# Forget attention on one core: a turn's dense filling in two parts instead of three

## The chip, the cores and the metric

One core of a Trainium2 chip runs the whole program in one launch. The metric is the time of that launch on the device in microseconds (us), as a median over runs. TensorE is called PE in the profile (PEld are its weight loads), VectorE DVE, ScalarE ACT, GpSimd POOL and SyncE SP.

## What is computed

Two blocks in a row on x of 1024 tokens by 1024 channels, in fp32: the first is a pooling mixer beside sliding-window attention, the second has eight heads of forgetting attention (causal, with a decay from cumulated log gates), eight heads of chunk-band attention, gates, and a feed-forward part. The change touches the two attentions of the second block and the projections that run between them:

```python
def forgetting_attention(q, k, v, log_f):
    c = jnp.cumsum(log_f, axis=-1)
    def block(args):
        qi, ci, i = args
        sc = jnp.einsum('bhqd,bhkd->bhqk', qi, k, preferred_element_type=jnp.float32)
        sc = sc * scale + ci[..., None] - c[:, :, None, :]
        sc = jnp.where(mask, sc, NEG)
        p = jax.nn.softmax(sc, axis=-1).astype(v.dtype)
        return jnp.einsum('bhqk,bhkd->bhqd', p, v)
...
def second_block(x, ...):
        h = rms_norm(x, norm1[l])
        proj = h @ w_in[l]
        qa, ka, va, fa, qc, kc, vc, gates = jnp.split(proj, SPLITS, axis=-1)
        o_a = from_heads(forgetting_attention(...))
        o_b = from_heads(chunk_band_attention(...))
        g_a, g_b = jnp.split(jax.nn.sigmoid(gates), N_BRANCH, axis=-1)
        merged = g_a * (o_a @ w_branch_a[l]) + g_b * (o_b @ w_branch_b[l])
        x = x + merged @ w_out[l]
        h2 = rms_norm(x, norm2[l])
        x = x + jnp.square(jax.nn.relu(h2 @ w_up[l])) @ w_down[l]
    return rms_norm(x, final_norm)
```

## The kernel before

**Precision.** A dense product is made of matmuls on halves: an operand is split into a high part (rounded to fp32r, by ScalarE) and a low part (the rest, by VectorE), and high x high, high x low and low x high are added in one PSUM bank. One *dense step* is such a group of three matmuls, 128x128 by 128x512, for one of eight slices of the inner dimension (`dense` is a generator that yields after each).

**The work of the attention.** The 16 heads are taken as eight pairs, 0 to 3 with the chunk band ("band pairs"), 4 to 7 with the causal mask and the forget gates ("causal pairs"). A *slot* is one head and one block of 128 queries, 128 in all; two slots make a `Step`, whose key blocks lie in groups of up to four blocks. A pair has 16 slots and 8 steps. `STEP_ORDER` is (3, 0, 2, 1): a step with many keys is followed by one with few.

**What sets TensorE's order.** The loop over *turns* in `tensor_program` writes it by hand. A turn holds

1. the scores of its slot (two fp32r matmuls for each part of up to four key blocks; in the causal pairs a small bf16 matmul adds the mask), into the banks 2 and 3 by turns;
2. filling, the first part (place 0);
3. the transposes (*turning*) of one visit's groups: `turn_weights` transposes up to four 128x128 blocks of the normed rows into the bank 5 or 6. It waits for `normed` (ScalarE scaled the rows) and for the low half (`plow`) of the group that had the bank before. A step's groups are turned in two visits, in two turns (`spread` is 2);
4. filling, the second part (place 1);
5. `products`: the groups turned in the turn before, times V, into the bank 4 or 7. They wait for those groups' `plow`;
6. filling, the third part (place 2).

The filling is the dense work of the next pairs' k, q and v and of three gates, from the generator `att_fill`. `take` adds a part of the turn's quota to a running credit and issues one dense step for each whole one. `att_quota` shares out 48 steps for a pair (37 for the last) over its slots by their number of keys. The transposes of v (`turn_v`) are issued inside a dense product.

**The other engines** follow the same turns, each in its own fixed order. ScalarE (`scalar_program`): the exponential of the turn's slot, the high half of the groups turned in this turn (`p_high`), the scaling (`normed`), half of a finished output, the evacuation of what dense work ended in this turn's three places, the high half of newly loaded weights. VectorE (`vector_program`): the low half of the groups turned in the turn before (`p_low`), add and maximum of the scores, an output, the low halves of k and q that ended in the turn before, the reciprocal (`one over`), the low half of weights. Both handle all that ended in a turn together, whatever its place.

**Names in the profile.** In this stretch dense matmuls read `b<-Yr,ringr`, scores `b<-Xr`, the mask `b<-maskb,identb`, products `b<-Wr,Xr`, transposes `b<-identf,Wf` (L93). `Wr<-b` on L97 is the high half of a turned group, `Wr<-b,Wr` on L101 its low half; `ringr<-stage` are the weights' halves; `Wf<-Wf,st` is the exponential on L98 and the scaling on L97; `Wf<-b,Wf` on L112 is the add with maximum; `st` are the small statistics.

Of the kernel before, what the change touches and what calls it, by code (L numbers as in the profile page):

```python
# [21 lines left out]
POOL_SLOT = (0, 1, 3, 2)  # L22
STEP_ORDER = (3, 0, 2, 1)
SLAB_OF_MERGED = (3, 1, 2, 4, 5, 6, 7, 0)
FILL = (0.3, 0.3, 0.4)
HALVES = ((0, 0), (1, 0), (0, 1))


# [510 lines left out]
def block(t):  # L539
    return slice(t * P, t * P + P)  # L540
# [11 lines left out]
def att_quota(slot):  # L552
    keys_of = band if slot.step.pair < 4 else causal
    total = 2 * sum(len(keys_of(i)) for i in range(NT))
    quanta = ATT_QUOTA if slot.step.pair < 7 else LAST_QUOTA
    return quanta * (len(slot.keys) + FIXED_KEYS) / (total + 16 * FIXED_KEYS)


def tensor_program(pe, m, at, note, units, swa, att):
# [125 lines left out]
    def take(steps, credit, quota):  # L685
        credit[0] += quota
        while credit[0] >= 1:
            credit[0] -= 1
            next(steps, None)

    def swa_fill():
        yield from dense("k", m.X, x_ready[1], 1, (0, 1))
        yield from dense("q0", m.X, x_ready[1], 1, (0, 1))
        yield from dense("ag0", m.X, x_ready[0], 0, (0, 1))
        yield from dense("v", m.X, x_ready[1], 1, (0, 1))
        for n in dense("ag0", m.X, x_ready[1], 1, (0, 1)):
            if n == 2:
                turn_v("s", m.vT1, 1)
            yield n
        for name in ("q1", "ag1", "q2", "ag2", "q3", "ag3", "u3", "pg3"):  # L700
            for h in range(2):
                yield from dense(name, m.X, x_ready[h], h, (0, 1))

    def turn_weights(stage, step, g, e_block, rooms, banks):
        b = banks[turn_count[0] % len(banks)]
        turn_count[0] += 1
        r = room_count[0] % len(rooms)
        room_count[0] += 1
        pe.wait_ge(*at["normed", stage, step.n])
        pe.wait_ge(*at[freed[b]])  # L710
        blocks = step.groups[g][0]
        for i, which in enumerate(blocks):
            sent = pe.transpose(m.banks[b][:, block(i)], e_block(step, which), m.identf[:])
        sent.then_inc(m.p_t, ("pturned", stage, step.n, g))
        note.bank["pturned", stage, step.n, g] = b
        note.room["pt", stage, step.n, g] = r
        note.room_free["pt", stage, step.n, g] = note.room.get(("pt", stage, r))
        note.room["pt", stage, r] = ("prod", stage, step.n, g)
        freed[b] = ("plow", stage, step.n, g)

    def products(stage, step, g, v_of, v_keys, rooms, base, b, room_free):
        pe.wait_ge(*at["plow", stage, step.n, g])
        if g == 0:
            for key in v_keys:
                pe.wait_ge(*at[key])
            pe.wait_ge(*at[room_free])
        r = rooms[note.room["pt", stage, step.n, g]]
        every = step.groups[g][1]
        for i, (key, c0, width, oc) in enumerate(every):
            for l in range(2):  # L730
                sent = pe.matmul(m.banks[b][:, base + oc:base + oc + width], v_of(key), r[:, l, c0:c0 + width],
                                 g == 0 and i == 0 and l == 0, g == len(step.groups) - 1 and i == len(every) - 1 and l == 1)
        sent.then_inc(m.p_v, ("prod", stage, step.n, g))
        note.bank["o", stage, step.n] = b

    place[0] = ("swa", -1, 0)
    credit = [0.0]
    steps = swa_fill()
    take(steps, credit, FIRST_STEPS)
    out_at = [0]  # L740
    for t, turn in enumerate(swa):
        quota = SWA_TAIL if turn.slot is None else FIRST_QUOTA if t < 4 else SWA_QUOTA
# [16 lines left out]
        place[0] = ("swa", t, 0)  # L759
        take(steps, credit, FILL[0] * quota)  # L760
        for step, g in turn.turned:
            def e_block(step, which):
                key, j = which
                i = step.n % 8
                at_ = j * 256 + (key - max(0, i - 1)) * P
                return m.e1[step.n % 3][:, at_:at_ + P]
            turn_weights("swa", step, g, e_block, m.pt1, TURN_BANKS)
        place[0] = ("swa", t, 1)
        take(steps, credit, FILL[1] * quota)
        for step, g in turn.applied:  # L770
# [8 lines left out]
        place[0] = ("swa", t, 2)  # L779
        take(steps, credit, FILL[2] * quota)  # L780
    place[0] = ("swa", len(swa), 0)
# [140 lines left out]
    def att_fill():  # L922
        names = [f"{x}2{n}" for n in range(1, 8) for x in "kqv"] + ["gb0", "ga0", "gb1"]
        valued = None
        for name in names:
            for h in range(2):
                for step in dense(name, m.Y, h2_ready[h], h, (0, 1)):
                    if valued is not None and step == 3:
                        turn_v(valued[0], m.vT2, valued[1])
                        valued = None  # L930
                    yield step
                if name[0] == "v":
                    valued = int(name[2]), h

    place[0] = ("att", -1, 0)
    steps = att_fill()
    credit = [0.0]
    take(steps, credit, LEAD)
    for t, turn in enumerate(att):
        quota = ATT_TAIL  # L940
        if turn.slot is not None:
            s = turn.slot
            n, j = s.step.pair, s.step.head
            quota = att_quota(s)
            q, k, _ = m.pair_rooms(n)
            for h in range(2):
                pe.wait_ge(*at["free", f"q2{n}", h])
                pe.wait_ge(*at["kdup", f"k2{n}", h])
            for x, ks in enumerate(s.parts):
                b = SCORE_BANKS[score_count[0] % 2]  # L950
                score_count[0] += 1
                pe.wait_ge(*at[freed[b]])
                kc = slice(ks[0] * P, ks[-1] * P + P)
                o = m.banks[b][:, 0:len(ks) * P]
                diag = n >= 4 and ks[-1] == s.i
                pe.matmul(o, q[:, j, block(s.i)], k[:, j, 0, kc], True, False)
                sent = pe.matmul(o, q[:, j, block(s.i)], k[:, j, 1, kc], False, not diag)
                if diag:
                    sent = pe.matmul(m.banks[b][:, block(len(ks) - 1)], m.identb[:], m.maskb[:], False, True)
                sent.then_inc(m.p_s, ("score", "att", s.n, x))  # L960
                note.bank["score", s.n, x] = b
                freed[b] = ("top", "att", s.n, x)
            if s.n == 111:
                ring.reached["att6_done"] = [("score", "att", s.n, len(s.parts) - 1)]
        place[0] = ("att", t, 0)
        take(steps, credit, FILL[0] * quota)
        for step, g in turn.turned:
            def e_block(step, which):
                key, jj = which
                keys_of = band if step.pair < 4 else causal  # L970
                first = keys_of(2 * step.a)
                c = first.index(key) if jj == 0 else len(first) + keys_of(2 * step.a + 1).index(key)
                return m.E2[0 if step.a >= 2 else 1][:, block(c)]
            turn_weights("att", step, g, e_block, m.pt2, ATT_TURN_BANKS)
        place[0] = ("att", t, 1)
        take(steps, credit, FILL[1] * quota)
        for step, g in turn.applied:
            v, j = m.pair_rooms(step.pair)[2], step.head
            products("att", step, g, lambda key: v[:, key, j, :, :].rearrange("p l c -> p (l c)"),
                     [("v", step.pair, h) for h in range(2)], m.pt2, 0, ATT_OUT_BANKS[step.n % 2],  # L980
                     ("oadd", "att", step.n - 2) if step.n > 1 else freed[ATT_OUT_BANKS[step.n % 2]])
            if g == len(step.groups) - 1:
                if step.n == 55:
                    ring.reached["v6_done"] = [("prod", "att", 55, g)]
        place[0] = ("att", t, 2)
        take(steps, credit, FILL[2] * quota)
        if turn.slot is None or turn.slot.step.pair == 7:
            ring.prepare(place[0], 1)
    for x in range(2):
# [1993 lines left out]
def build(nc, x, w_in, pool_w, pool_scale, attn_sinks, w_out, norm_pre, norm_post, norm1_2, w_in_2,  # L2983
# [11 lines left out]
    for program in (tensor_program, scalar_program, vector_program, gpsimd_program, sync_program):  # L2995
        program(Lane(None, at), m, at, note, units, swa, att)
# [50 lines left out]
```

## Time and profile before

| what | value |
|---|---|
| median of 3 runs | 1842.23 us (1841.41 to 1843.25) |
| the profiled execution, own time | 1841.51 us |
| its span, first to last instruction | 1839.4 us |
| PE busy | 1814.0 us, 99% of the span, 8937 matmuls |
| PEld busy | 1507.7 us, 82% |
| DVE busy | 1158.0 us, 63% |
| ACT busy | 922.2 us, 50% |
| chain that ended last, share on PE | 87% |
| mean granted clock of TensorE | 0.998 |

The chain is followed back from the last instruction, at each step to what released it. "Busy" adds up the intervals in which an engine works; of a matmul the start is measured and the end is modelled, and neighbours overlap, so TensorE's pace is read from start to start. In the timeline, equal instructions in a row are merged to one line with their count, and a bracket at the end is the idle time ahead of it with what released it. The attention of the second block runs from about 413 to 900 us.

### The profile page before, as it was taken

Reading aid. Unit: us, or ns where it says so; the run is one execution under the profiler, and the core shown is the slowest. Engines: PE = TensorE matmul, PEld = TensorE weight load, DVE = VectorE, ACT = ScalarE, POOL = GpSimd, SP = SyncE. Lnnn points to the kernel's source line nnn. Section 1 sums busy time; section 2 is a strip of 40 time slices with the busy share of each in tenths; the row PEclk is TensorE's granted clock in tenths of the full one; section 3 lists DMA queues with packets and bytes.
Section 4 is the critical chain, followed back from the end, with each engine's and each line's share of the span. In section 5 each row is a group of like instructions: output and inputs, shape, how many; then the busy total and the mean of one; then the engine's idle time right before and its main releaser. Section 6 shows DMA issues by size and latency. Waiting matters only on the chain.

```text
span 1839.4 us, 23494 instructions
## 1 busy us (share of the span) xinstructions
PE 1814.0 (99%) x8937; PEld 1507.7 (82%) x8937; DVE 1158.0 (63%) x2220; ACT 922.2 (50%) x1629; POOL 90.8 (5%) x165
## 2 busy tenths in 40 slices
PE   8999999999999999999999999999999999999998
PEld 6888888878888888887888888888888888888887
DVE  5788854546666666666532224488665567687877
ACT  5556433347777777777511114245555555433343
POOL 4111100000000000000000000000000000000000
PEclk9999999999999999999999999999999999999999
DMA  5411115333222223122321114324445367554422
GB/s 173 127 35 30 47 46 161 110 88 84 69 72 54 64 76 78 54 66 78 92 55 46 51 53 137 115 75 144 148 145 168 129 216 259 183 186 170 177 96 115
DMA packets 160034, 196.41 MB, mean 107 GB/s; under 512 B 9441, under 2 KB 114473, under 8 KB 156466
## 3 DMA queue, kind: packets, MB, share of 16 engines
q1 hardware_dynamic: 154034, 182.30, 30.8%
q0 software_dynamic: 5888, 12.62, 3.0%
q8 instruction: 70, 1.15, 0.3%
q14 instruction: 42, 0.34, 0.1%
HBM read 139.25 MB, written 49.34 MB: 103 GB/s over the span
## 4 chain that ended last, share of the span: by engine, by line
PE 87%; DVE 6%; ACT 3%; issue 2%; DMA 0%; POOL 0%; SPq 0%; DVEq 0%; POOLq 0%; ACTq 0%
PE b L86 64%; PE b L90 19%; PE b L93 4%; DVE Wf L112 1%; DVE Wr L101 1%; ACT Wf L98 1%; DVE ringr L101 1%; ACT Wf L97 1%; DVE Xr L101 1%; ACT Xr L97 1%; ACT Wr L97 1%; ACT ringr L97 0%; DMA stage<-in_w_in_dram 0%; DVE Wf L101 0%; DVE st L119 0%
## 5 line engine op out<-in xcount | busy, mean ns | idle before, releaser
L86 PE MATMUL b<-Yr,ringr 128*128 128x512 f32 x1920 | 507.7, 400 | 0.0
L86 PE MATMUL b<-Xr,ringr 128*128 128x512 f32 (+1 forms) x1608 | 390.5, 390 | 0.9 <-DVE Wr L101 0.6
L86 PEld LDWEIGHTS b<-Yr,ringr 128*128 128x128 f32 x1920 | 340.3, 189 | 54.4
L86 PEld LDWEIGHTS b<-Xr,ringr 128*128 128x128 f32 x1608 | 292.4, 189 | 56.0 <-issue 1.2
L98 ACT ACTIVATE Wf<-Wf,st 128x640 f32<-128x640 f32 (+3 forms) x192 | 125.2, 652 | 162.6 <-DVE st L116 66.0
L101 DVE TENSOR_TENSOR Wf<-Wf,b 128x512 f32<-128x512 f32 x160 | 108.6, 684 | 117.1 <-PE b L86 70.2
L101 DVE TENSOR_TENSOR ringr<-stage,ringr 128x1024 fp32r<-128x1024 f32 x79 | 97.2, 1234 | 134.3 <-ACT ringr L97 133.9
L112 DVE CUSTOM_DVE_ANT_0 Wf<-b,Wf 128x256 f32<-128x256 f32 (+3 forms) x256 | 118.3, 490 | 70.2 <-PE b L86 69.8
L97 ACT ACTIVATE Wf<-b 128x512 f32<-128x512 f32 (+3 forms) x231 | 114.9, 498 | 86.0 <-PE b L86 60.5
L86 PE MATMUL b<-Xr 128*128 128x512 f32 (+3 forms) x672 | 150.3, 354 | 0.0
L86 PEld LDWEIGHTS b<-Xr 128*128 128x128 f32 x672 | 123.0, 188 | 21.3
L93 PE MATMUL b<-identf,Wf 128*128 128x128 f32 (+1 forms) x809 | 119.2, 275 | 10.8 <-DVE Wr L101 5.1
L101 DVE TENSOR_TENSOR Wr<-b,Wr 128x512 fp32r<-128x512 f32 (+2 forms) x186 | 112.8, 624 | 25.1 <-ACT Wr L97 22.4
L93 PEld LDWEIGHTS b<-identf,Wf 128*128 128x128 f32 (+1 forms) x809 | 94.5, 140 | 41.3 <-ACT Wf L97 12.2
L97 ACT ACTIVATE Wf<-Wf 128x512 f32<-128x512 f32 (+1 forms) x114 | 71.2, 625 | 107.7 <-DVE Wf L101 104.8
L86 PE MATMUL b<-Yr,Xr 128*128 128x512 f32 x528 | 123.3, 391 | 0.0
L97 ACT ACTIVATE ringr<-stage 128x1024 fp32r<-128x1024 f32 x80 | 84.1, 1055 | 66.6 <-PE b L86 62.8
L86 PEld LDWEIGHTS b<-Yr,Xr 128*128 128x128 f32 x528 | 98.7, 188 | 20.3
L97 ACT ACTIVATE Wf<-Wf,st 128x640 f32<-128x640 f32 (+7 forms) x128 | 93.9, 733 | 9.2 <-DVE st L119 9.0
L97 ACT ACTIVATE Wr<-b 128x512 fp32r<-128x512 f32 (+2 forms) x186 | 95.4, 535 | 5.5 <-PE b L93 4.3
L86 PEld LDWEIGHTS b<-Wr,Xr 128*128 128x128 f32 x608 | 86.0, 189 | 8.1
L97 ACT ACTIVATE Xr<-b 64x512 fp32r<-64x512 f32 (+1 forms) x108 | 62.9, 592 | 52.4 <-PE b L93 39.9
(174 smaller groups left out, 2453.8 us busy)
## 6 DMA issues: line engine op xcount, KB each, us to landing
stage<-in_w_in_dram SPq DMA_DIRECT2D x58, 512.0 KB, 4.0
scratch_u<-Wf SPq DMA_DIRECT2D x80, 256.0 KB, 4.1
Wf<-scratch_u SPq DMA_DIRECT2D x14, 1024.0 KB, 4.7
stage<-scratch_u SPq DMA_DIRECT2D x13, 1024.0 KB, 4.8
stage<-in_w_up_dram SPq DMA_DIRECT2D x24, 512.0 KB, 4.3
stage<-in_w_out_dram SPq DMA_DIRECT2D x16, 512.0 KB, 3.5
scratch_x<-Wf SPq DMA_DIRECT2D x16, 512.0 KB, 2.7
Xr<-Xr POOLq DMA_DIRECT2D x32, 256.0 KB, 3.4
```

What stands on the lines that cost most here:

```text
L86: return self.send(lambda e: e.matmul(o, w, a, start=start, stop=stop))
L90: return self.send(lambda e: e.matmul(o, w, a, start=False, stop=stop, skip_group_check=True))
L93: return self.send(lambda e: e.transpose(o, a, ident))
L97: return self.send(lambda e: e.activation(o, a, fn, bias=bias, scale=scale))
L98: return self.send(lambda e: e.activation(o, a, fn, bias=bias, scale=scale, accum_out=acc))
L101: return self.send(lambda e: e.tensor_tensor(out=o, in0=a, in1=b, op=op))
L112: return self.send(lambda e: e.tensor_tensor_reduce(out=o, in0=a, in1=b, scale=1.0, scalar=LOWEST, op0=ALU.add, op1=ALU.max, accum_out=top))
```

## The change

In the attention of the second block (`att`) the filling of a turn has two parts: 0.6 of the quota ahead of the transposes, none between transposes and products, 0.4 behind the products. The first block's attention (`swa`) keeps `FILL`. The middle place still exists, but nothing is issued in it.

```diff
--- before.py
+++ after.py
@@ -22,7 +22,7 @@
 POOL_SLOT = (0, 1, 3, 2)
 STEP_ORDER = (3, 0, 2, 1)
 SLAB_OF_MERGED = (3, 1, 2, 4, 5, 6, 7, 0)
-FILL = (0.3, 0.3, 0.4)
+FILL, ATT_FILL = (0.3, 0.3, 0.4), (0.6, 0.4)
 HALVES = ((0, 0), (1, 0), (0, 1))
 
 
@@ -963,7 +963,7 @@
             if s.n == 111:
                 ring.reached["att6_done"] = [("score", "att", s.n, len(s.parts) - 1)]
         place[0] = ("att", t, 0)
-        take(steps, credit, FILL[0] * quota)
+        take(steps, credit, ATT_FILL[0] * quota)
         for step, g in turn.turned:
             def e_block(step, which):
                 key, jj = which
@@ -973,7 +973,6 @@
                 return m.E2[0 if step.a >= 2 else 1][:, block(c)]
             turn_weights("att", step, g, e_block, m.pt2, ATT_TURN_BANKS)
         place[0] = ("att", t, 1)
-        take(steps, credit, FILL[1] * quota)
         for step, g in turn.applied:
             v, j = m.pair_rooms(step.pair)[2], step.head
             products("att", step, g, lambda key: v[:, key, j, :, :].rearrange("p l c -> p (l c)"),
@@ -983,7 +982,7 @@
                 if step.n == 55:
                     ring.reached["v6_done"] = [("prod", "att", 55, g)]
         place[0] = ("att", t, 2)
-        take(steps, credit, FILL[2] * quota)
+        take(steps, credit, ATT_FILL[1] * quota)
         if turn.slot is None or turn.slot.step.pair == 7:
             ring.prepare(place[0], 1)
     for x in range(2):
```

On TensorE this moves instructions. In the band pair 1, around two turns (a dense step is `b<-Yr,ringr` x3), the order was:

```order
L86 MATMUL b<-Xr 128x128 x2
L93 MATMUL b<-identf,Wf 128x128 x8
L86 MATMUL b<-Yr,ringr 128x512 x3
L86 MATMUL b<-Wr,Xr 128x256 x2
L86 MATMUL b<-Wr,Xr 128x128 x2
L86 MATMUL b<-Xr 128x256 x2
L86 MATMUL b<-Yr,ringr 128x512 x3
L93 MATMUL b<-identf,Wf 128x128 x2
L86 MATMUL b<-Yr,ringr 128x512 x3
L86 MATMUL b<-Wr,Xr 128x256 x8
```

and at the same place it is now:

```order
L86 MATMUL b<-Xr 128x128 x2
L86 MATMUL b<-Yr,ringr 128x512 x3
L93 MATMUL b<-identf,Wf 128x128 x8
L86 MATMUL b<-Wr,Xr 128x256 x2
L86 MATMUL b<-Wr,Xr 128x128 x2
L86 MATMUL b<-Xr 128x256 x2
L86 MATMUL b<-Yr,ringr 128x512 x6
L93 MATMUL b<-identf,Wf 128x128 x2
L86 MATMUL b<-Wr,Xr 128x256 x8
```

In both turns one dense step went from behind the transposes to ahead of them. The distance from the scores to the products stays.

In the causal pair 4, around the second visit of a step (three transposes), the order was:

```order
L93 MATMUL b<-identf,Wf 128x128 x7
L86 MATMUL b<-Yr,ringr 128x512 x3
L86 MATMUL b<-Wr,Xr 128x256 x8
L86 MATMUL b<-Xr 128x384 x2
L86 MATMUL b<-Xr 128x256 x2
L86 MATMUL b<-maskb,identb 128x128
L86 MATMUL b<-Yr,ringr 128x512 x3
L93 MATMUL b<-identf,Wf 128x128 x3
L86 MATMUL b<-Yr,ringr 128x512 x3
```

and at the same place it is now:

```order
L86 MATMUL b<-Yr,ringr 128x512 x3
L93 MATMUL b<-identf,Wf 128x128 x7
L86 MATMUL b<-Wr,Xr 128x256 x8
L86 MATMUL b<-Xr 128x384 x2
L86 MATMUL b<-Xr 128x256 x2
L86 MATMUL b<-maskb,identb 128x128
L86 MATMUL b<-Yr,ringr 128x512 x6
L93 MATMUL b<-identf,Wf 128x128 x3
```

Six dense matmuls stand ahead of the three transposes instead of three, and products follow each turning at once. TensorE has as many matmuls as before, and VectorE, ScalarE, GpSimd and SyncE have the same instructions in the same order.

## Rows read from the trace of the kernel before

**Rows 1.** Busy us by stretch: PE, PEld, DVE, ACT, POOL; clock, DMA share, GB/s.
```profile
413.00:895.00 482.00, 472.48 (x2759) 400.05 (x2758) 323.82 (x951) 358.03 (x713) 17.95 (x40) 1.00 0.26 69
895.00:1800.00 905.00, 905.00 (x4031) 749.88 (x4031) 531.64 (x578) 352.64 (x435) 5.60 (x8) 1.00 0.40 135
```

**Rows 2.** Waits of TensorE, 421 to 896 us: total, times, longest.
```profile
PE b L93 <- DVE Wr L101: 5.1, 12, 1.1
PE b L93 <- ACT Wf L97: 3.6, 6, 1.5
```

**Rows 3.** Timeline: start, length (us), engine, line, operation, count, idle before.
```profile
709.22 0.86 PE L86 MATMUL b<-Yr,ringr 128*128 128x512 f32 x3
709.92 0.97 PE L86 MATMUL b<-Xr 128*128 128x512 f32 x4
...
712.60 0.95 PE L86 MATMUL b<-Yr,ringr 128*128 128x512 f32 x3
713.38 0.58 PE L86 MATMUL b<-Wr,Xr 128*128 128x256 f32 x4
713.79 1.37 PE L86 MATMUL b<-Yr,ringr 128*128 128x512 f32 x5
```

**Rows 4.** Timeline, PE: products right behind transposes.
```profile
720.85 1.04 PE L93 MATMUL b<-identf,Wf 128*128 128x128 f32 x8
721.64 0.66 PE L86 MATMUL b<-Wr,Xr 128*128 128x256 f32 x4
722.14 0.91 PE L86 MATMUL b<-Yr,ringr 128*128 128x512 f32 x3
```

**Rows 5.** Timeline, PEld: weight loads of transposes behind narrow scores.
```profile
423.46 0.64 PEld L93 LDWEIGHTS b<-identf,Wf 128*128 128x128 f32 x6 [1.47 <-ACT Wf L97]
...
451.42 0.42 PEld L93 LDWEIGHTS b<-identf,Wf 128*128 128x128 f32 x4 [0.15 <-ACT Wf L97]
...
481.12 0.85 PEld L93 LDWEIGHTS b<-identf,Wf 128*128 128x128 f32 x8 [0.31 <-ACT Wf L97]
```

**Rows 6.** Timeline, PE and DVE, around two second visits of a step.
```profile
438.95 0.86 PE L86 MATMUL b<-Yr,ringr 128*128 128x512 f32 x3
440.02 0.44 PE L93 MATMUL b<-identf,Wf 128*128 128x128 f32 x2 [0.21 <-DVE Wr L101]
...
439.27 1.29 DVE L101 TENSOR_TENSOR Wr<-b,Wr 128x512 fp32r<-128x512 f32 x2
...
468.19 0.84 PE L86 MATMUL b<-Yr,ringr 128*128 128x512 f32 x3
...
469.16 0.44 PE L93 MATMUL b<-identf,Wf 128*128 128x128 f32 x2
```

**Rows 7.** Timeline, DVE and PEld: a turn's second group of transposes.
```profile
451.65 0.56 DVE L101 TENSOR_TENSOR Wr<-b,Wr 128x384 fp32r<-128x384 f32 x1
...
452.26 0.42 PEld L93 LDWEIGHTS b<-identf,Wf 128*128 128x128 f32 x4 [0.42 <-DVE Wr L101]
```

**Rows 8.** Timeline, PE and DVE: the long wait of the pair 4.
```profile
662.83 0.95 PE L86 MATMUL b<-Yr,ringr 128*128 128x512 f32 x3
...
664.02 1.16 DVE L101 TENSOR_TENSOR Wr<-b,Wr 128x512 fp32r<-128x512 f32 x2
...
664.85 0.52 PE L93 MATMUL b<-identf,Wf 128*128 128x128 f32 x3 [1.08 <-DVE Wr L101]
```

**Rows 9.** Timeline, PE and ACT: the largest wait, in the pair 7.
```profile
858.51 0.94 PE L86 MATMUL b<-Yr,ringr 128*128 128x512 f32 x3
...
859.94 0.93 ACT L97 ACTIVATE Wf<-Wf,st 128x768 f32<-128x768 f32 x1 [0.64 <-DVE st L119]
...
860.93 1.09 PE L93 MATMUL b<-identf,Wf 128*128 128x128 f32 x8 [1.48 <-ACT Wf L97]
```

**Rows 10.** Timeline, DVE and PE: products with the least to spare.
```profile
675.38 1.29 DVE L101 TENSOR_TENSOR Wr<-b,Wr 128x512 fp32r<-128x512 f32 x2
...
676.53 1.19 PE L86 MATMUL b<-Wr,Xr 128*128 128x256 f32 x8
```

## The prediction

> **What bounds the kernel now.** I read the page first. TensorE is busy for 1814.0 us of 1839.4, and the chain of waits lies on it for 87%. Then the busy times by stretch [rows 1]: in the forget attention (413 to 895 us) TensorE is busy for 472.5 of 482 us, and after it for every one of the 905 us up to 1800. So the stretch that the change touches is bound by TensorE, with some gaps. Whatever they give back reaches the end in full, since nothing behind them stands idle that could swallow it. VectorE and ScalarE are busy for 324 and 358 of the 482 us. They follow TensorE, but where their work is bunched they can lead it.
>
> The waits of TensorE in the stretch come next [rows 2]: all of them stand ahead of transposes (L93). Twelve are for a low half that VectorE writes (`plow`, which frees the turning bank), six for rows that ScalarE has normed (`normed`). None is ahead of a score, a product or a dense step. These idle times are short of the real loss: a matmul's end is modelled, so I measure from start to start.
>
> The measure is the timeline of TensorE [rows 3, 4]. Three dense matmuls, one step of the filling, take 0.70 us (709.22 to 709.92). Right behind transposes they take 0.78 (712.60 to 713.38). Four products of 256 columns take 0.41 behind a dense step and 0.50 right behind transposes.
>
> **What the change does.** Before, a turn's filling stood at three places: 0.3 ahead of the transposes, 0.3 between them and the products, 0.4 behind. Now the middle part stands ahead of the transposes. With a quota of 1.4 to 4.6 steps (48 shared out by keys), most turns move exactly one step of three matmuls; where the running credit rounds otherwise, none. No matmul is added or dropped. The other engines keep their order; only some semaphore waits of ScalarE fall away, because TensorE's events come in another order. No DMA is added or moved past another on SP's or POOL's queue.
>
> *The issue itself.* Before: a dense step 0.70, eight transposes 0.79, a dense step 0.78, four products 0.41, in sum 2.68. Now: two steps 1.40, transposes 0.79, products 0.50, in sum 2.69 [rows 3, 4]. About 75 turns change so: nothing gained, nothing lost, 0 us, with 0.01 x 75 = 0.8 either way.
> A rule speaks against this move. The Trainium skill (TensorE: Matmul & The Clock Gate, LDWEIGHTS) gives the loading of a 128-column operand as columns over 1.2, an estimate of 107 ns, and says elsewhere on the page that it hides under the matmul in flight. Were it laid bare at each new place where products follow transposes, 75 times, that would be 8.0 us more. The trace has 20 such places already, and the one shown has 0.09 more for the products and 0.08 less for the dense step that no longer follows transposes. I go by the rows.
>
> *A: transposes that wait for the normed rows.* The weight loads of transposes come late behind a pair of 128-column scores [rows 5]: 1.47 us once at the start, 0.15 in four places (451.42 the first), 0.31 in three (481.12 the first), in sum 3.0. The length from a score over VectorE's add, the exponential, the reciprocal and the scaling to `normed` does not hang on the filling; the copy of the turned group that stands ahead of the scaling on ScalarE comes behind the exponential anyway. The transposes now stand one step, 0.70, further from the score. The small ones go whole (0.60 + 0.93) and the first shrinks by 0.70. Gain 2.2.
>
> *B: the first transposes of a step's second visit, in the four band pairs.* They wait for the low half of the group turned a visit earlier [rows 6]: the three matmuls ahead of them last 1.07 in place of 0.70 (438.95 to 440.02), four times, and 0.97 (468.19 to 469.16), four times: 4 x 0.37 + 4 x 0.27 = 2.5. The distance from one turning to the next does not change, so a low half that came straight from its turning would be just as late. But this one stands in VectorE's queue: it starts at 439.27 right behind other work. That queue is tied to scores and dense ends, which stay. I take the whole 2.5; below it is 0.
>
> *C: the second group of transposes inside a turn, four times.* Its weight load is 0.42 late, and the low half it waits for starts at 451.65 after other VectorE work [rows 7]. A step more ahead would cover it, but the turn before (A) has the same cover spent already, and TensorE, earlier from A and B, meets VectorE at its busiest. I take 0; bounds 0 and 1.7.
>
> *D: three causal pairs, one long wait each.* From 662.83 to 664.85 three dense matmuls and a wait take 2.02, that is 1.3 too much. The low half starts at 664.02, behind weight work on VectorE [rows 8]. One more step there shortens each wait by 0.70. Gain 2.1.
>
> *E: the last pair.* The largest wait, 1.6 (858.51 to 860.93 is 2.42, less 0.78), follows ScalarE's scaling at 859.94 [rows 9]. The order of TensorE at this place is the same before and now, so it stays; smaller ones nearby may go, and TensorE comes earlier to this one, which gives them back. I take 0, bounds 1 us either way.
>
> *What is late next.* The products lose that same step. Ahead of them the tightest place has two low halves from 675.38, done at 676.67; the second four products start halfway through the eight, at about 677.04, so 0.37 to spare [rows 10]. Less 0.70 this is a wait of 0.33, if the low half does not move. There are three such places (the pairs 4, 5, 6): 1.0 us, and all of TensorE's later work stands behind them. Scores lose nothing against their own adds, but the low half goes ahead of the next add on VectorE; with no wait of a score in the list [rows 2] I put that at nothing, and if that cover is gone it is the last rival.
>
> Sum: 2.2 + 2.5 + 0 + 2.1 + 0 - 1.0 = 5.8 us. The profiled execution took 1841.51 (span 1839.4 and 2.1 around it), so 1835.7; the median of the runs is 0.7 above it: **1836.4 us**.
>
> **The rivals.**
> 1. *Only A is gained.* The waits for low halves are waits for one of two turning banks, and one turning to the next stays the same distance. For it: twelve of eighteen waits are of this kind. Against it: the low half at 439.27 is held by its queue. Then 1842.2 - 2.2 = 1840.0. The Trainium skill (Perfetto Trace Analysis, Optimization Strategy) reads the same gap repeating on the engine that should be full as a sign of too few buffers; by that, no move of filling cures B and D.
> 2. *All of it is gained*: C's 1.7 too and no wait of the products, 5.8 + 1.7 + 1.0 = 8.5, so 1833.7. Against it: in bunches ScalarE and VectorE work without a pause, and TensorE cannot outrun them.
> 3. *A bare weight load at the new handovers.* Loads of transposes follow each other at 0.11 (eight in 0.85) [rows 5]; one bare at each new place is 75 x 0.11 = 8.2, less the 5.8, so 1844.6. Against it: rows 4.
> 4. *The products take over the waiting: slower.* If each low half follows its transposes rigidly, 0.70 later, then every step of the pairs 0 to 6 with as little to spare as in rows 10 waits 0.33. With 17 of the 56 steps the gain is gone, with 29 the kernel is slower by over 0.2%; all 56 cost 18.5, so 1855. For some 36 steps, 12 - 5.8: 1848.5. Against it: no product waits now, and low halves wait for VectorE more than for their transposes.
>
> **How the numbers follow.** 0.2%, or 3.7 us, is about what a measurement of this kernel tells from no change. Chances: forecast 0.61, rival 1 0.22, rival 2 0.10, rival 3 0.02, rival 4 0.05. The range takes in B's and E's bounds on the forecast and reaches to rivals 1 and 2: 1832.5 to 1841.5. Faster by over 0.2% is below 1838.5: most of the forecast (0.55), rival 2 and a little of rival 1, in sum 0.69. Within: 0.06 of the forecast, most of rival 1 and half of rival 3, 0.25. Slower: 0.06.
>
> **What would show it.** In the profile after: TensorE's waits in the stretch fall from 18 places to about 10; no transposes late behind 128-column scores except the first, by about 0.8; the three long waits about 0.6 instead of 1.3; the wait at 861 us still there; some new waits of products for VectorE's low half, short. The stretches behind 900 us look the same, only earlier. I am wrong if the products' waits add up to more than 2 us, or if the transposes' waits keep their lengths, or if an idle stretch turns up after 900 us.

## The result and the profile after

The change makes the kernel faster: 1831.86 us, median of 5 runs (1831.26 to 1832.99), against 1841.89 of the kernel before (1840.59 to 1843.25). The ratio is 0.9949, with a 95% interval of 0.9938 to 0.9960. That is 10 us where 5.8 were forecast. The time lies 0.6 under the lower end of the range.

From the page of the changed kernel: the busy row and the chain that ended last.

```profile
PE 1810.6 (99%) x8937; PEld 1506.6 (82%) x8937; DVE 1157.4 (63%) x2220; ACT 923.2 (50%) x1629; POOL 90.8 (5%) x165
...
PE 92%; DVE 3%; ACT 2%; issue 1%; DMA 0%; SPq 0%; POOL 0%; POOLq 0%; DVEq 0%; ACTq 0%
```

TensorE is busy for 3.4 us less, in a span that is 9.6 shorter, and the chain now lies on it for 92%, not 87%. VectorE's share of the chain fell from 6 to 3% and ScalarE's from 3 to 2%. The waiting that went had been handed to TensorE by these two. A matmul's end is modelled, so busy sums mix pace and waiting. I go on from start to start.

The windows of the changed kernel that answer to [rows 1], moved with the program:

```profile
413.50:886.00 472.50, 468.61 (x2758) 399.21 (x2757) 321.94 (x950) 358.03 (x712) 17.94 (x40) 1.00 0.26 69
886.00:1790.00 904.00, 903.99 (x4026) 748.59 (x4025) 531.71 (x578) 352.54 (x435) 5.60 (x8) 1.00 0.40 135
```

In the attention TensorE stood idle for 9.5 us and now for 3.9. Behind it, it has no gap, as before. The waits of TensorE in the same stretch, the answer to [rows 2]:

```profile
PE b L93 <- ACT Wf L97: 2.3, 2, 1.7
PE b L93 <- DVE Wr L101: 1.3, 4, 0.3
```

Eighteen waits with 8.7 us became six with 3.6. One of the six, 1.7 us, stands in the last pair and is longer than it was (1.5 in [rows 9]).

**Where the time went.** The kernel has the same 8937 matmuls, and outside the attention in the same order, so the start of the n-th can be set against the start of the n-th. From the 1987th (408.23 us before, 407.49 after), which lies ahead of the attention, to the 4833rd (909.00 and 899.35), which lies behind it, it is 500.8 us before and 491.9 after: 8.9 less. From there to the last matmul it is 923.47 and 923.43: nothing given back, nothing gained. The remaining 0.7 of the span's 9.6 arises ahead of the attention, where the order is the same. It is the program's start, which varies from run to run (last section). Of the 8.9, 5.5 are gained by the first mask matmul of the pair 4 (647.33 before), so in the four band pairs, 2.9 between there and the pair 7's first (837.55), 0.5 behind it.

The filling moved at 87 of the 123 places where transposes stand, each time by one dense step. At the other 36 the running credit had reached no whole step in the middle part, and TensorE's order there is the old one. Products stood directly behind transposes at 20 places and now do at 95.

Each place of the forecast, by the same measure:

| term of the forecast | forecast us | measured us |
|---|---|---|
| issue itself, the new handovers | 0 | 0 |
| A, first transposes | 0.70 | 0.70 |
| A, three places of 0.31 | 0.93 | 1.0 |
| A, four places of 0.15, with C behind them | 0.60 + 0 | 0.7 |
| B, second visits in the band pairs | 2.5 | 2.8 |
| D, three long waits | 2.1 | 2.2 |
| small waits inside a group of seven transposes, pairs 4 to 6 | none | 0.7 |
| E, last pair, a late product in it | 0 | 0.5 |
| products late, pairs 4 to 6 | -1.0 | 0 |
| sum | 5.8 | 8.6 |

The other 0.3 of the 8.9 are in pieces too small to give to a place.

B in the changed kernel, the place of [rows 6], timeline of VectorE and TensorE:

```profile
437.48 1.52 PE L86 MATMUL b<-Yr,ringr 128*128 128x512 f32 x6
...
438.31 1.29 DVE L101 TENSOR_TENSOR Wr<-b,Wr 128x512 fp32r<-128x512 f32 x2
...
439.06 0.44 PE L93 MATMUL b<-identf,Wf 128*128 128x128 f32 x2
```

TensorE's last matmul ahead of the transposes begins at about 438.62 (six dense from 437.48, 0.228 apart), so 0.44 before them. At full pace it would be 0.23. A wait of 0.21 is left of 0.37 once; at the other seven places none is left. The low half still starts late in VectorE's queue (438.31), but TensorE has more in front of it.

D in the changed kernel, the place of [rows 8]:

```profile
656.54 1.22 DVE L101 TENSOR_TENSOR ringr<-stage,ringr 128x1024 fp32r<-128x1024 f32 x1
...
656.65 1.64 PE L86 MATMUL b<-Yr,ringr 128*128 128x512 f32 x6
...
657.80 1.16 DVE L101 TENSOR_TENSOR Wr<-b,Wr 128x512 fp32r<-128x512 f32 x2
...
658.64 0.52 PE L93 MATMUL b<-identf,Wf 128*128 128x128 f32 x3 [0.34 <-DVE Wr L101]
...
658.91 1.14 PE L86 MATMUL b<-Wr,Xr 128*128 128x256 f32 x8
```

Six dense matmuls stand there where three did. From 656.65 to 658.64 is 1.99 us; six at full pace take 1.48 there, and 0.51 is left of 1.25. VectorE still takes a 1.22-us weight half (656.54) ahead of the low half. TensorE now spends 0.7 us of that time on a dense step.

### The profile page after: what moved, and what is told of

It reads as the page before. It is cut to its first block, busy times and chain, and to the rows that moved or that the text cites. A ratio compares the mean times of both kernels' runs of the same rounds, so it can differ in the third digit from the quotient of the medians.

```text
span 1829.8 us, 23494 instructions
## 1 busy us (share of the span) xinstructions
PE 1810.6 (99%) x8937; PEld 1506.6 (82%) x8937; DVE 1157.4 (63%) x2220; ACT 923.2 (50%) x1629; POOL 90.8 (5%) x165
## 4 chain that ended last, share of the span: by engine, by line
PE 92%; DVE 3%; ACT 2%; issue 1%; DMA 0%; SPq 0%; POOL 0%; POOLq 0%; DVEq 0%; ACTq 0%
PE b L86 69%; PE b L90 19%; PE b L93 5%; DVE Wr L101 1%; ACT Wf L98 1%; DVE Wf L112 1%; ACT Xr L97 0%; DMA stage<-in_w_in_dram 0%; ACT Wf L97 0%; DVE ringr L101 0%; ACT Wr L97 0%; ACT ringr L97 0%; DVE Wf L105 0%; DVE Xr L101 0%; DVE Yr L109 0%
## 5 line engine op out<-in xcount | busy, mean ns | idle before, releaser
L86 PE MATMUL b<-Yr,ringr 128*128 128x512 f32 x1920 | 491.4, 397 | 0.0
L86 PEld LDWEIGHTS b<-Yr,ringr 128*128 128x128 f32 x1920 | 345.1, 189 | 60.0
L86 PE MATMUL b<-Yr,Xr 128*128 128x512 f32 x528 | 123.3, 390 | 0.0
L86 PE MATMUL b<-Wr,Xr 128*128 128x256 f32 (+1 forms) x608 | 94.1, 288 | 0.0
L90 PE MATMUL b<-Yr,Xr 128*128 128x512 f32 x384 | 88.3, 389 | 0.0
```

Of the source, the lines that this page charges most:

```text
L86: return self.send(lambda e: e.matmul(o, w, a, start=start, stop=stop))
L90: return self.send(lambda e: e.matmul(o, w, a, start=False, stop=stop, skip_group_check=True))
```

## The experiments

Each kernel is the one before with one edit, the last one is the changed kernel with one. The first seven change only the parts of a turn's filling, for all turns of the attention or for some. Their times are compared with runs of the kernel before on the same chip (median 1841.37 of 21 for the first four, 1841.62 of 27 for the others). "The attention" is the stretch between the two matmuls named above, 500.8 us before and 491.9 with the change.

**Two parts, but the middle one behind the products.** The change leaves two parts and puts one step more ahead of the transposes. This kernel does only the first of the two.

```diff
+        fill = (0.3, 0.0, 0.7)
-        take(steps, credit, FILL[0] * quota)
+        take(steps, credit, fill[0] * quota)
...
-        take(steps, credit, FILL[1] * quota)
+        take(steps, credit, fill[1] * quota)
...
-        take(steps, credit, FILL[2] * quota)
+        take(steps, credit, fill[2] * quota)
```

> The forget attention's middle part of the filling goes behind the products (0.3, 0, 0.7) instead of ahead of the transposes. The turn has two parts as in the change, and products right behind the transposes. Cover theory (time comes only from dense work that stands ahead of transposes which would wait): the transposes stand where they stood, so their waits stay; 0 us gained against before, up to 2 us lost where products meet a low half earlier. Handover theory (two parts instead of three save issue time by themselves): 3 to 9 us faster than before.

Measured: 1841.06 us (11 runs), ratio 0.9998 (0.9989 to 1.0007), attention 500.7. Its waits:

```profile
PE b L93 <- DVE Wr L101: 5.4, 12, 1.1
PE b L93 <- ACT Wf L97: 3.8, 7, 1.5
```

These are the waits of [rows 2] with one more, 9.2 us in place of 8.7. The products follow the transposes at once in the same 95 places as in the change, and it is worth nothing (0.1 us by the attention). What the change gives comes from the step ahead of the transposes, and the new handovers neither cost nor give anything that can be told.

**The mirror: nothing ahead of the transposes.**

```diff
+        fill = (0.0, 0.6, 0.4)
```

> The first part of the filling goes from ahead of the transposes to between them and the products (0, 0.6, 0.4), the mirror of the change: transposes stand one dense step nearer to the scores. Cover theory: each of about 19 waits of the transposes grows by up to 0.70 us and new ones appear, so slower than before by 13 us or more. Handover theory: as many places with products right behind transposes as before or fewer, so within 2 us of before.

Measured: 1857.84 us (4 runs), ratio 1.0089 (1.0076 to 1.0103), attention 517.2, so 16.4 longer. Its waits:

```profile
PE b L93 <- DVE Wr L101: 14.8, 21, 1.7
PE b L93 <- ACT Wf L97: 7.6, 13, 2.0
```

Taking the filling away from the transposes costs 16.4, adding to it gives 8.9. The two are not quite mirrors: here one step went at 73 places and two at 21, where the change added one at 87. Even so a step taken away costs more than a step added gives, since a wait grows with each step that is missing but can only be taken down to nothing.

**The band pairs alone, and the causal pairs alone.**

```diff
+        fill = (0.6, 0.0, 0.4) if turn.turned and turn.turned[0][0].pair < 4 else FILL
```

> The change in the band pairs 0 to 3 alone; the causal pairs keep three parts. Cover theory: the gain of the terms A and B, by the trace of the changed kernel about 5 us (between the starts of the attention and of the pair 4 it had won 5.1 us). If the terms were of the size that the prediction gave them: 4.7. A rival, that the pairs 0 to 3 only pass their waits on to the causal pairs: 0 to 2 us in sum.

Measured: 1835.76 us (5 runs), ratio 0.9968 (0.9956 to 0.9981), attention 495.5. The waits:

```profile
PE b L93 <- DVE Wr L101: 3.5, 4, 1.1
PE b L93 <- ACT Wf L97: 2.4, 3, 1.5
```

```diff
+        fill = FILL if turn.turned and turn.turned[0][0].pair < 4 else (0.6, 0.0, 0.4)
```

> The change in the causal pairs 4 to 7 alone; the band pairs keep three parts. Cover theory: three long waits lose 0.7 each and smaller ones go, about 3.5 us faster than before (the trace of the changed kernel won 3.8 us from the pair 4 on). By the prediction's terms, D less the products' wait: 1.1 us faster. With e3 the sum should be the whole, 8.9 us, if the halves do not depend on each other.

Measured: 1837.99 us (11 runs), ratio 0.9983 (0.9974 to 0.9991), attention 497.3. The waits:

```profile
PE b L93 <- ACT Wf L97: 3.6, 5, 1.7
PE b L93 <- DVE Wr L101: 2.9, 12, 0.4
```

The two give 5.6 and 3.4 us by the medians, 9.0 in sum, and 5.3 and 3.4 by the attention, 8.7 of the 8.9. Each part of the attention earns its own share, and the band pairs don't pass their waits on. The first list keeps D's long waits (1.1). The second keeps all twelve places of [rows 2], and D's three have shrunk to 0.4 at most.

**The first visits of a step alone, and the second visits alone.**

```diff
+        fill = (0.6, 0.0, 0.4) if turn.turned and turn.turned[0][1] == 0 else FILL
```

> The change (0.6, 0, 0.4) only in turns that turn a step's first visit, three parts in all others. This is where the transposes wait for normed rows (term A). If A is a thing of its own: 2.2 us faster than before by the prediction's rows, 2.9 by the spacing in the trace of the changed kernel. Rival: first and second visits are tied, a first turning that comes 0.7 later makes its low half late for the second visit, whose transposes have not moved; then the waits of B and D grow and the sum is near 0 or slower.

Measured: 1838.26 us (11 runs), ratio 0.9983 (0.9974 to 0.9991), attention 497.2. Two places of its timeline on TensorE:

```profile
425.13 0.85 PE L86 MATMUL b<-Yr,ringr 128*128 128x512 f32 x3
426.04 0.44 PE L93 MATMUL b<-identf,Wf 128*128 128x128 f32 x2
...
438.97 0.85 PE L86 MATMUL b<-Yr,ringr 128*128 128x512 f32 x3
440.31 0.44 PE L93 MATMUL b<-identf,Wf 128*128 128x128 f32 x2 [0.48 <-DVE Wr L101]
```

A and D are gained here. But B grew: from 438.97 to 440.31 is 1.34 where it was 1.07 [rows 6], so its first wait is 0.64, not 0.37. Three more of B's places grew by 0.03 to 0.07, and four stayed. At 426.04 stands a wait of 0.21 (0.91 from 425.13, not 0.70) that is neither in the kernel before nor in the changed one; there are five such places, of 0.21 to 0.25. A step that comes ahead of the first visit lets TensorE run up to the second visit earlier, where the low half comes hardly sooner.

```diff
+        fill = FILL if turn.turned and turn.turned[0][1] == 0 else (0.6, 0.0, 0.4)
```

> The change only in turns that turn a step's second visit (and in those that turn none). This holds B and D: 4.6 us faster than before by the prediction's terms, 4.9 by the trace of the changed kernel; with e5 it should make 8.9 if the two kinds of turn do not depend on each other, and they must not be added if e5 comes out near 0.

Measured: 1837.44 us (11 runs), ratio 0.9978 (0.9969 to 0.9987), attention 497.1, so 3.7 less where 4.9 were expected. B is gone, and D's long waits are all there (1.20 to 1.21 by start to start, 1.25 before). The expectation had put D among the second visits, as does the text ahead of the prediction, and this corrects both: the three transposes of D are the first and only visit of the next step. They wait for the low half of the group that had their bank, the third of the step before; it is the first of the two groups that the turn before had turned. In sum the two kernels give 7.2 of the 8.9 (3.5 and 3.7 by the attention). The pairs add up, the visits don't: the five new waits and the growth of B in the kernel above come to 1.6 us, about what is missing. With the step ahead of both visits these are covered too.

**More ahead still.**

```diff
+        fill = (0.9, 0.0, 0.1)
```

> Nine tenths of the filling ahead of the transposes, one tenth behind the products. If cover ahead of the transposes were all that counts, the long waits left (three of 0.5, one of 0.8) would go: 2 to 3 us faster than the change. Rival: the other ends of the turn have a limit too. The turned copy stands ahead of the scaling on ScalarE, so transposes that come later make the next normed rows later, and v that is turned inside the filling meets dense work that waits for it; then the time is given back and the kernel is 2 to 6 us slower than before.

Measured: 1839.65 us (11 runs), ratio 0.9992 (0.9983 to 1.0000), attention 499.1. Neither expectation came: it is 7.2 us longer than the change in the attention and still 1.7 shorter than before. Its waits, and a group of transposes in its timeline:

```profile
PE b L93 <- ACT Wf L97: 4.4, 7, 1.1
PE b L86 <- DVE Xr L101: 1.9, 6, 0.3
PE b L93 <- DVE Wr L101: 1.3, 4, 0.3
PE b L86 <- DVE Wr L101: 0.7, 1, 0.7
```

```profile
452.04 1.14 PE L93 MATMUL b<-identf,Wf 128*128 128x128 f32 x6 [0.64 <-ACT Wf L97]
```

D keeps its 0.51. What comes new are a dense step that waits for turned v (`Xr`), six times; transposes that wait 0.8 for normed rows in each band pair (452.04), where the step behind the products, ahead of the scores, is gone (that this is the reason is argued, not shown); and one wait of products, 0.7 in the list. So products that wait, the forecast's "what is late next", exist, but in one place, near the end of the last pair. The changed kernel has the same wait there with 0.27:

```profile
889.92 0.54 PEld L86 LDWEIGHTS b<-Wr,Xr 128*128 128x128 f32 x4 [0.43 <-DVE Wr L101]
```

There the dense step that stood between the transposes and the products did move ahead.

**VectorE's low halves before its other work.** C's waits are left in the changed kernel: eight transposes with 0.11 ahead of the first and 0.20 in the middle.

```profile
449.23 1.23 DVE L101 TENSOR_TENSOR ringr<-stage,ringr 128x1024 fp32r<-128x1024 f32 x1
...
450.40 1.35 PE L93 MATMUL b<-identf,Wf 128*128 128x128 f32 x8
...
450.49 0.56 DVE L101 TENSOR_TENSOR Wr<-b,Wr 128x384 fp32r<-128x384 f32 x1
...
451.10 0.42 PEld L93 LDWEIGHTS b<-identf,Wf 128*128 128x128 f32 x4 [0.28 <-DVE Wr L101]
```

The second four wait for a low half that starts at 450.49, right behind the low half of loaded weights (449.23). This kernel is the changed one, with the low half of those weights (`att_split`) put behind the next turn's `p_low` in one turn of eight, up to turn 110.

```diff
+def LATE_LOW(t):
+    return t % 8 == 0 and t < 110
...
+        if t > 1 and LATE_LOW(t - 2):
+            att_split(t - 2)
...
-        if t and not taken:
+        if t and not taken and not LATE_LOW(t - 1):
             att_split(t - 1)
...
-        if taken:
+        if taken and not LATE_LOW(t - 1):
             att_split(t - 1)
```

> The change, and on VectorE the low half of loaded weights is moved behind the low half of turned groups in every eighth turn (the turn whose number divides by 8, up to 110). If the wait of term C (0.35 to 0.42 before, 0.2 in the changed kernel, four times, and its neighbour of 0.1) is set by VectorE's queue, it goes: 1 to 2 us faster than the change. If it were set by the number of turning banks or by the turning itself, nothing changes.

Measured: 1832.26 us (5 runs), ratio to the kernel before 0.9952 (0.9938 to 0.9965), attention 491.6. Beside the change's 1831.86 no difference can be told, where 1 to 2 us were expected. Its timeline at the same place (line numbers are higher by 5):

```profile
449.82 0.56 DVE L106 TENSOR_TENSOR Wr<-b,Wr 128x384 fp32r<-128x384 f32 x1 [0.35 <-ACT Wr L102]
...
450.56 1.09 PE L98 MATMUL b<-identf,Wf 128*128 128x128 f32 x8
...
451.41 0.65 PE L91 MATMUL b<-Wr,Xr 128*128 128x256 f32 x4
...
452.96 1.29 DVE L106 TENSOR_TENSOR Wr<-b,Wr 128x512 fp32r<-128x512 f32 x2 [0.32 <-ACT Wr L102]
...
453.70 0.44 PE L98 MATMUL b<-identf,Wf 128*128 128x128 f32 x2
```

The low half starts at 449.82, and the eight transposes take 0.85 to the products (450.56 to 451.41) where they took 1.11. The wait of C was VectorE's order. But the next pair of transposes, at 453.70, now waits 0.12, since the low half ahead of it (452.96) comes no sooner: it stands behind its own high half on ScalarE. Per band pair 0.2 is gained and some 0.12 given back; 0.2 remain of the whole attention. No kernel beat the change by more than that.

## Why the prediction was wrong, and where right

**The mechanism was right.** The time comes from a step of filling that stands ahead of the transposes and covers their wait. A measured 2.4 us for 2.2 and D 2.2 for 2.1. The waits left of the two are 0.75 and 0.51 where "about 0.8" and "about 0.6" were forecast, and the 923 us behind the attention kept their length. The first experiment takes the other half of the edit by itself and finds nothing in it.

**The step that failed is "What is late next".** It took 1.0 us off for products in three places which "lose that same step". At those places there was none to lose. In the kernel before, the rows just ahead of the products of [rows 10] are

```profile
676.29 0.49 PE L93 MATMUL b<-identf,Wf 128*128 128x128 f32 x3
```

and in the changed kernel

```profile
668.48 1.29 DVE L101 TENSOR_TENSOR Wr<-b,Wr 128x512 fp32r<-128x512 f32 x2
...
669.40 0.49 PE L93 MATMUL b<-identf,Wf 128*128 128x128 f32 x3
...
669.64 1.20 PE L86 MATMUL b<-Wr,Xr 128*128 128x256 f32 x8
```

The three transposes stood right ahead of the products before the change too (676.29, then 676.53); the turn's middle part was empty there, because the credit had not reached a whole step. It is one of the 36 places where nothing moved. From the transposes to the products it is 0.24 us in both. The low halves start 0.91 ahead of the transposes before (675.38 to 676.29) and 0.92 after (668.48 to 669.40), since VectorE's queue is tied to the scores. So the 0.37 to spare stayed. I had the products' spare time from a row, but took the lost step from the rule that "most turns move exactly one step", without looking whether this turn was one of them. In the whole attention only one place of products waits, in the last pair (889.92, by 0.27): there the step between transposes and products was lost as the forecast said, and the wait is near the 0.33 that it named.

**Waits that the list does not show** were left out of the sum. The forecast counted what the list of waits and a few timelines showed. In the pairs 4 to 6, three groups of seven transposes were late inside the group, without a bracket in the timeline. Before:

```profile
691.59 1.15 PE L93 MATMUL b<-identf,Wf 128*128 128x128 f32 x7
692.49 0.70 PE L86 MATMUL b<-Yr,ringr 128*128 128x512 f32 x2
```

After:

```profile
685.33 0.93 PE L93 MATMUL b<-identf,Wf 128*128 128x128 f32 x7
686.01 0.72 PE L86 MATMUL b<-Wr,Xr 128*128 128x256 f32 x4
```

From the first of the seven to the next matmul it was 0.90 and is 0.68. Three times this is 0.7 us. A comparison of starts with the pace of the same pair of instructions elsewhere would have shown them beforehand.

**B was 0.3 too low** (2.8 against 2.5). Four times 0.37 and four times 0.27 are 2.56, not 2.5, and 0.2 of it is still there. The rest stood behind: after a late transpose the next one came late too. From 440.02 two of them took 0.19 to the next dense step (440.21), at full pace 0.14. I had counted only what stood ahead of the first.

**E** was "0, bounds 1 us either way" and came out at 0.5. The large wait did stay, and grew to 1.87 from 1.64, as TensorE comes earlier to it; four smaller ones at 852, 875, 888 and 894 us went, 1.0 in sum, and the products' 0.27 came. What holds the large one is ScalarE's queue:

```profile
847.25 1.05 ACT L97 ACTIVATE Xr<-stage 128x1024 fp32r<-128x1024 f32 x1
...
848.20 1.05 ACT L97 ACTIVATE ringr<-stage 128x1024 fp32r<-128x1024 f32 x1
...
849.14 0.92 ACT L98 ACTIVATE Wf<-Wf,st 128x768 f32<-128x768 f32 x1
...
850.80 0.94 ACT L97 ACTIVATE Wf<-Wf,st 128x768 f32<-128x768 f32 x1 [0.64 <-DVE st L119]
...
851.79 1.09 PE L93 MATMUL b<-identf,Wf 128*128 128x128 f32 x8 [1.70 <-ACT Wf L97]
```

Two weight halves of 1.05 us each (847.25 and 848.20) go ahead of the exponential at 849.14, and the transposes can only start behind the scaling (850.80). Filling doesn't change this. Moving the two behind the exponential was not tried.

**C** was taken at 0 and is within 0.1 of it. Its reason, that the cover is spent in the turn before, was not tested by itself. The last experiment shows that the wait is VectorE's, and that half of what is won there is asked for again one turn later.

**The handovers** cost nothing, as taken from rows. At a place of the last pair, the kernel before and then the changed one:

```profile
894.84 0.94 PE L86 MATMUL b<-Yr,ringr 128*128 128x512 f32 x3
895.62 0.57 PE L86 MATMUL b<-Wr,Xr 128*128 128x256 f32 x4
896.03 1.14 PE L86 MATMUL b<-Yr,ringr 128*128 128x512 f32 x4
```

```profile
885.23 0.66 PE L93 MATMUL b<-identf,Wf 128*128 128x128 f32 x4
885.64 0.66 PE L86 MATMUL b<-Wr,Xr 128*128 128x256 f32 x4
886.13 2.28 PE L86 MATMUL b<-Yr,ringr 128*128 128x512 f32 x9
```

Four products took 0.41 behind a dense step (895.62 to 896.03) and take 0.49 behind transposes (885.64 to 886.13). The dense step that had 0.78 behind transposes (894.84 to 895.62) is now one at full pace. +0.08 and -0.08. The Trainium skill (TensorE: Matmul & The Clock Gate, LDWEIGHTS) puts a 128-column load, were it laid bare, at an estimated 107 ns; by these rows none is.

**The rivals.** Rival 1 (only A) fell: B and D came. The Trainium skill (Perfetto Trace Analysis, Optimization Strategy) says that a gap that repeats can mean too few buffers. Here the gap repeated eight times in the band pairs and three times behind them. With two turning banks as before it went at seven of the eight, and shrank from 1.25 to 0.51 at the three: the measurement decides against the conclusion that no move of filling cures B and D. Whether a third turning bank would have cured them too was not tried. Rival 3 fell with the rows above, rival 4 with the list of waits, which has none of TensorE's products in the pairs 0 to 6. Rival 2 (1833.7) is nearest to the time. Of the 2.7 by which it exceeded the forecast, the 1.0 of the products came and C's 1.7 did not; the small waits, E and B stand in its place. The range ended at 1832.5, as it took nothing in for waits that no list shows.

The rest of the difference is no effect of the change. 8.9 us in the attention make 1832.6 from the profiled 1841.51, and the program's start and the medians' scatter account for the last 0.7. From the median of 1842.23 that the forecast started from, 8.9 would have made 1833.3, inside the range. So that the time fell just below the range is partly chance; that the gain was 8.9 and not 5.8 is not.

## What to carry to other kernels

Where an in-order engine is the bound and its order is written by hand, independent work belongs directly ahead of the instruction that waits, and how much is best depends on what is left behind: here 0.6 of a turn's filling, where 0.3 had stood, gave 8.9 us, 0.9 gave 1.7, and none cost 16.4. Before charging a loss to a place, look in the order of the program at that very place whether what is said to leave it was ever there. Sum the waits from start-to-start distances against the normal pace: the list of waits fell by 5.1 us where the stretch lost 8.9, and three places worth 0.7 were never in it.

## What the runs showed of the hardware

- The program's start varies more than anything behind it: the 400th matmul begins between 83.3 and 85.7 us over the ten profiled kernels, whose orders up to there are the same, while the 923.4 us behind the attention agree within 0.07. A change of one or two microseconds in a late stage is read from that stage's two ends and not from the whole time.
- Moving transposes next to products and dense matmuls away from transposes shifts 0.08 us from one neighbour to the other and leaves the sum as it is.
